# One-hot shares of an expert layer as rounded 256-column matmuls, and rounded operands in the attention scores

## The reference

```python
def one_block(args):            # attention, one block of 128 queries
    s = jnp.einsum('bhqd,bhkd->bhqk', q_blk, k).astype(jnp.float32) * scale
    s = s + c_blk[..., None] - cum[:, :, None, :]      # cum: running sum of log forget gates
    s = jnp.where(key_pos[None, :] <= q_pos[:, None], s, -jnp.inf)
    p = jax.nn.softmax(s, axis=-1)
...
s_top, i_top = lax.top_k(scores, PEER_TOPK)            # per token and head, 2 x 16 of 128 keys
...
expert_idx = jnp.take_along_axis(cand_i, pos, axis=-1) # 128 picks a token out of 128*128 experts
gates = jax.nn.softmax(best_s, axis=-1)
u_sel = u_tab[i_blk]
act = jax.nn.gelu(jnp.einsum('td,thkd->thk', h_blk, u_sel).astype(jnp.float32))
w = (g_blk * act).astype(h.dtype)
return jnp.einsum('thk,thkd->td', w, v_tab[i_blk])
```

## Time and profile before

| | |
|---|---|
| median of 3 runs | 3398.49 us (3394.14 to 3400.37) |
| profiled execution, its own time | 3398.76 us |
| its span in the trace | 3397.0 us |
| PE busy | 3303.0 us, 97% of the span |
| DVE, ACT, POOL busy | 59%, 32%, 13% |
| matmul records | 14716 |

### The profile page before, as it was taken

How to read it: one execution, slowest core, us unless ns; L and a number is a source line. 1 busy time by engine, 2 the same in 40 slices (tenths; PEclk the granted TensorE clock), 3 DMA queues, 4 the chain that set the end, 5 groups by cost and what they waited for, 6 DMA issues and landing times.

```text
span 3397.0 us, 37999 instructions
## 1 busy us (share of the span) xinstructions
PE 3303.0 (97%) x14716; PEld 2584.0 (76%) x14716; DVE 1998.6 (59%) x3778; ACT 1070.5 (32%) x1393; POOL 429.9 (13%) x186
## 2 busy tenths in 40 slices
PE   7998999989999899999989999999999999999999
PEld 6876778768777556765668888888888788888887
DVE  6678343447888789345535858566631255555554
ACT  3265222233222311234333233455542211111111
POOL 0000000014031000000002444322234100000000
PEclk9999999999999899999999999999999999999999
DMA  5144324323332333220123344388885555555553
GB/s 196 59 136 134 99 69 142 131 68 94 105 124 90 136 109 104 77 81 25 44 75 103 130 140 140 121 194 190 196 211 179 183 188 190 190 188 186 186 188 116
DMA packets 280948, 451.58 MB, mean 133 GB/s; under 512 B 147776, under 2 KB 154048, under 8 KB 280512
## 3 DMA queue, kind: packets, MB, share of 16 engines
q1 hardware_dynamic: 145152, 405.10, 36.4%
q10 hardware_dynamic: 135616, 44.04, 6.1%
HBM read 369.39 MB, written 79.69 MB: 132 GB/s over the span
## 4 chain that ended last, share of the span: by engine, by line
PE 92%; DVE 6%; ACT 1%; issue 1%; DMA 0%; POOL 0%; ACTq 0%; DVEq 0%
PE psum L588 92%; DVE wl L1372 1%; ACT wh L981 1%; DVE trigw L1469 0%; DVE yb L1583 0%; DVE psum L1725 0%; DVE lb L1574 0%; DVE trig L1470 0%; DVE trig L1465 0%; DVE cs L1581 0%; DVE y L1585 0%; DVE n L1508 0%; DVE trig L1467 0%; DVE trig L1468 0%; DVE trigw L1466 0%
## 5 line engine op out<-in xcount | busy, mean ns | idle before, releaser
L588 PE MATMUL psum<-h_hi,wh 128*128 128x512 f32 x2144 | 865.9, 404 | 45.2 <-DVE wl L1372 16.1
L1372 DVE TENSOR_TENSOR wl<-ring,wh 128x1024 fp32r<-128x1024 f32 (+2 forms) x320 | 373.6, 1171 | 850.2 <-ACT wh L981 849.3
L588 PE MATMUL psum<-h_hi,wl 128*128 128x512 f32 x2144 | 851.4, 397 | 0.0
L588 PE MATMUL psum<-h_lo,wh 128*128 128x512 f32 x2144 | 850.1, 396 | 0.0
L981 ACT ACTIVATE wh<-ring 128x1024 fp32r<-128x1024 f32 (+2 forms) x492 | 504.1, 1026 | 834.2 <-PE psum L588 813.4
L2055 POOL TENSOR_TENSOR wl<-ring,wh 128x1024 fp32r<-128x1024 f32 x172 | 426.2, 2479 | 1913.8 <-ACT wh L981 1913.8
L588 PEld LDWEIGHTS psum<-h_hi,wh 128*128 128x128 f32 x2144 | 406.3, 190 | 149.6 <-issue 54.1
L588 PEld LDWEIGHTS psum<-h_hi,wl 128*128 128x128 f32 x2144 | 405.7, 189 | 100.4
L588 PEld LDWEIGHTS psum<-h_lo,wh 128*128 128x128 f32 x2144 | 406.5, 190 | 92.8 <-issue 1.9
L588 PE MATMUL psum<-ews_hi,wl 128*128 128x512 f32 x1024 | 408.6, 399 | 0.0
L588 PE MATMUL psum<-ews_lo,wh 128*128 128x512 f32 x1024 | 403.5, 394 | 0.0
(11 more groups left out here) (367 smaller groups left out, 3825.2 us busy)
## 6 DMA issues: line engine op xcount, KB each, us to landing
ring<-tables SPq DMA_DIRECT2D x256, 512.0 KB, 3.7
acts_scratch<-ga SPq DMA_DIRECT2D x128, 256.0 KB, 2.2
gates_scratch<-stage ACTq DMA_DIRECT2D x8, 4096.0 KB, 26.7
abuf<-acts_scratch SPq DMA_DIRECT2D x128, 256.0 KB, 3.9
gbuf<-gates_scratch SPq DMA_DIRECT2D x128, 256.0 KB, 4.2
ring<-w_up SPq DMA_DIRECT2D x44, 512.0 KB, 3.6
ring<-w_modb SPq DMA_DIRECT2D x32, 512.0 KB, 3.7
statew<-states_scratch SPq DMA_DIRECT2D x16, 640.0 KB, 3.8
```

What stands on the lines that cost most here:

```text
L588: return nc.tensor.matmul(out, lhsT, rhs, start=first, stop=last, **kw)
L1372: TT(wl, slot(t, 0, size[t]), wh.bitcast(F32), ALU.subtract).then_inc(S("low_by_ve"), 1)
```

## The change

The change has these parts.

1. **Spreads.** SPREAD_AT goes from 56 to 46, SPREADS from 3 to 2, PICKS_AT to (21, 29, 36, 44). The one-hots become fp32r and unscaled, and both sets come from one DVE instruction of 1024 elements (`hots_of`). The shares are split into a rounded high part (`picks_hi`) and the rest (in `picksT`); ACT scales the one-hots of key b by both, sixteen ACTIVATEs of 128x128 for a tile (`shares_of`), into `hbg`, 256 columns a token. PE does four rounded matmuls of 256 columns for a spread, which fill two banks. DVE sums the two halves of each from PSUM into the staging tile (`stage_gates`, a reduce of 1024 elements to 512) in place of ACT's copy. ACT issues the write of a full staging tile one `ui` tile later (`park_gates`).
2. **Scores.** `cumn` is split on DVE into two rounded rows of a zeroed tile `cums`; SP moves the second by a small transfer to partitions 32 to 39; `pick_head` (128x8, a one at rows h and 32+h) stands, broadcast, for `sel`. `mask` and `ident` get rounded copies. So the second and third matmul of each block of scores are fp32r.
3. **Order in the attention loop.** `head_sum` of head hd+2 is issued behind the scores of head hd+1 instead of ahead, and writes an H bank.
4. `bank(b)` is shifted by one bank, so that the two banks of a spread stand side by side.

```diff
-SPREAD_AT, SPREADS = 56, 3
-PICKS_AT = (28, 36, 45, 54)
+SPREAD_AT, SPREADS = 46, 2
+PICKS_AT = (21, 29, 36, 44)
...
-    if _u + 2 < HEADS:
-        head_sums(HEADS + _u + 2)
     if _u + 1 < HEADS:
         scores(_u + 1)
+    if _u + 2 < HEADS:
+        head_sums(HEADS + _u + 2, "H")
...
         def bank(b, n=T):
-            return psum[:, b % NBK, 0:n]
+            return psum[:, (b + 1) % NBK, 0:n]
...
             stream("vv", "w_v2", 8)
+            sp.wait_ge(S("cum_ready"), 1)
+            sp.dma_start(cums[32:32 + HEADS, :].bitcast(F32), cum_lo[0:HEADS, :].bitcast(F32)).then_inc(S("cum_moved"), 16)
...
-                if j == SPREAD_AT + T // 4 // SPREADS + 10:
+                if j == SPREAD_AT + T // 4 // SPREADS + 6:
...
                     mm(bank(b, nk), qT[:, hd, qb * P:(qb + 1) * P], kT[:, hd, 0:nk], True, False)
-                    mm(bank(b, nk), sel[0:HEADS, hd, :], cumn[:, 0:nk], False, False)
-                    mm(bank(b)[:, qb * P:nk], ident[:, :], maskt[:, :], False, True).then_inc(PE, 1)
+                    mm(bank(b, nk), pick_head[:, hd:hd + 1].to_broadcast([P, P]), cums[:, 0:nk], False, False)
+                    mm(bank(b)[:, qb * P:nk], ident_r[:, :], mask_r[:, :], False, True).then_inc(PE, 1)
...
-                if hd + 2 < HEADS:
-                    head_sum(HEADS + hd + 2)
                 if hd + 1 < HEADS:
                     scores(hd + 1)
+                if hd + 2 < HEADS:
+                    upper_free(pe, HIGH[f"hs{HEADS + hd + 2}"])
+                    pe.wait_ge(S("hsq_ready"), HEADS + hd + 3)
+                    mm(upper(HIGH[f"hs{HEADS + hd + 2}"]), ones[:, :], ht[:, hd % 2, :], True, True).then_inc(PE, 1)
...
             def spread(n):
-                b = BLOCK[f"ui{SPREAD_AT + n // SPREADS}"] + n % SPREADS
-                block_free(pe, b)
-                pe.wait_ge(S("hot_ready"), n + 1)
-                for k in range(4):
-                    last = mm(bank(b)[:, k * P:(k + 1) * P], hot_a[:, n % 4, k * P:(k + 1) * P],
-                              hot_b[:, n % 4, k * P:(k + 1) * P], True, True)
-                last.then_inc(PE, 1)
+                b = spread_block(n)
+                for k in range(2):
+                    block_free(pe, b + k)
+                    pe.wait_ge(S("shares_ready"), 4 * n + 2 * k + 2)
+                    for q in range(2):
+                        last = mm(bank(b + k)[:, 2 * P * q:2 * P * (q + 1)], hots[n % 3][:, 2 * k + q, :],
+                                  hbg[n % 3][k][:, q, :], True, True)
+                    last.then_inc(PE, 1)
...
+            def shares_of(n):
+
+                act.wait_ge(S("hot_ready"), n + 1)
+                for q in range(4):
+                    t, one = 4 * n + q, hots[n % 3][:, 4 + q, :].bitcast(F32)
+                    to = hbg[n % 3][q // 2][:, q % 2, :]
+                    A(to[:, 0:P], one, ACT.Copy, scale=picks_hi[:, t:t + 1].bitcast(F32))
+                    A(to[:, P:2 * P], one, ACT.Copy, scale=picksT[:, 2, t:t + 1]).then_inc(S("shares_ready"), 1)
...
-                for n in SPREAD_OF[j]:
-                    gate_stage(n)
+                if j + 1 < PK:
+                    for n in SPREAD_OF[j + 1]:
+                        shares_of(n)
+                for n in SPREAD_OF[j - 1]:
+                    park_gates(n)
...
-            v.tensor_tensor_scan(cumn, ones[0:HEADS, 0:1].to_broadcast([HEADS, T]), fl[2], 0.0, ALU.mult, ALU.add)\
-                .then_inc(S("cum_ready"), 1)
+            link(v.tensor_tensor_scan(cumn, ones[0:HEADS, 0:1].to_broadcast([HEADS, T]), fl[2], 0.0, ALU.mult, ALU.add))
+            ve.wait_ge(S("cum_zero"), 1)
+            link(v.tensor_copy(cums[0:HEADS, :], cumn))
+            TT(cum_lo[0:HEADS, :], cumn, cums[0:HEADS, :].bitcast(F32), ALU.subtract).then_inc(S("cum_ready"), 1)
...
+            def hots_of(n):
+                if n >= 3:
+                    block_here(ve, spread_block(n - 3) + 1)
+                both_picks = picksT[:, 0:2, 4 * n:4 * n + 4].unsqueeze(3).to_broadcast([P, 2, 4, P])
+                TT(hots[n % 3].rearrange("p (k q) j -> p k q j", k=2),
+                   rows.unsqueeze(1).unsqueeze(1).to_broadcast([P, 2, 4, P]), both_picks, ALU.is_equal)\
+                    .then_inc(S("hot_ready"), 1)
+
+            def stage_gates(n):
...
+                block_here(ve, b + 1)
+                sums = psum[:, (b + 1) % NBK:(b + 1) % NBK + 2, :].rearrange("p b (q k j) -> p (b q) j k", k=2, j=P)
+                v.tensor_reduce(parked[g % 2][:, :, t0:t0 + 4].rearrange("p j t -> p t j"), sums, AX, ALU.add)\
+                    .then_inc(S("gates_staged"), 1)
...
+                hots_of(n)
+                if n >= 2:
+                    stage_gates(n - 2)
```

More of the change, by code:

```diff
@@ L143, in head_rows, with head_sums @@
     stage(f"hs{n}", ["B"], False, lambda k: ("qk_normed", n + 1))
-def head_sums(n):
-    stage(f"hs{n}", ["B"], False, lambda k: ("ksd_done", n - HEADS + 1))
+def head_sums(n, bank="B"):
+    stage(f"hs{n}", [bank], False, lambda k: ("ksd_done", n - HEADS + 1))
 for _u in range(NS):
@@ L190 @@
     else:
-        stage(f"ui{_j}", ["T"] + ["B"] * len(SPREAD_OF[_j]), True,
-              lambda k, j=_j: ("gates_staged", SPREAD_OF[j][k] + 1))
+        stage(f"ui{_j}", ["T"] + ["B"] * (2 * len(SPREAD_OF[_j])), True,
+              lambda k, j=_j: ("gates_staged", SPREAD_OF[j][k // 2] + 1))
 for _v in range(PK):
@@ L374, in build @@
         eq, prod = (ar(n, B + 16400 + k * 2048, 1, 2048)[:, 0, :] for k, n in enumerate(("eq", "prod")))
-        picksT = ar("picksT", B + 20496, 3)
-        hot_a, hot_b = ar("hot_a", B + 16400, 4), ar("hot_b", B + 18448, 4)
+        picksT = ar("picksT", B + 20496, 4)
+        picks_hi = ar("picks_hi", B + 22032, 1, T, F32R)[:, 0, :]
+        hots = [ar(f"hots{k}", at, 8, P, F32R) for k, at in enumerate((B + 16400, B + 17424, B + 22544))]
+        hbg = [[ar(f"hbg{k}_{j}", at, 2, 2 * P, F32R) for j, at in enumerate(ats)] for k, ats in
+               enumerate(((B + 18448, B + 18960), (B + 19472, B + 19984), (B + 23568, B + 26128)))]
         parked = [ar(f"stage{k}", B + k * PK * TG, PK, TG) for k in range(2)]
@@ L1202, in head_root @@
             def head_root(n):
-                b = BLOCK[f"hs{n}"]
-                block_here(act, b)
+                if n >= HEADS + 2:
+                    upper_here(act, HIGH[f"hs{n}"])
+                    sums = upper(HIGH[f"hs{n}"])
+                else:
+                    block_here(act, BLOCK[f"hs{n}"])
+                    sums = bank(BLOCK[f"hs{n}"])
                 act.wait_ge(S("qk_normed"), max(n - 1, HEADS))
-                A(ht[:, 2 + n % 2, :], bank(b), ACT.Sqrt, scale=1.0 / P, bias=epsc).then_inc(S("ksd_done"), 1)
+                A(ht[:, 2 + n % 2, :], sums, ACT.Sqrt, scale=1.0 / P, bias=epsc).then_inc(S("ksd_done"), 1)
             def to_head(name, n, upper_bank=False):
@@ L1321, in key_copy, with park_gates @@
                 A(scb[:, n % 4, :], bank(b), ACT.Copy).then_inc(S("sc_ready"), 1)
[L1323 to L1330, removed]
-                if t0 == TG - 4:
+            def shares_of(n):
[5 more added lines that the diff above has]
+                    A(to[:, P:2 * P], one, ACT.Copy, scale=picksT[:, 2, t:t + 1]).then_inc(S("shares_ready"), 1)
+            def park_gates(n):
+                g, last = n // (TG // 4), n % (TG // 4) == TG // 4 - 1
+                if last:
                     act.wait_ge(S("gates_staged"), n + 1)
@@ L1985, in _ @@
             ve.wait_ge(S("iota_turned"), 1)
-            def spread(n):
-                if n >= 4:
-                    block_here(ve, BLOCK[f"ui{SPREAD_AT + (n - 4) // SPREADS}"] + (n - 4) % SPREADS)
-                TT(t3(hot_b[:, n % 4, :], P), rows.unsqueeze(1).to_broadcast([P, 4, P]),
-                   picksT[:, 1, 4 * n:4 * n + 4].unsqueeze(2).to_broadcast([P, 4, P]), ALU.is_equal)
-                for q in range(4):
-                    t = 4 * n + q
-                    last = TS(hot_a[:, n % 4, q * P:(q + 1) * P], rows, picksT[:, 0, t:t + 1], picksT[:, 2, t:t + 1],
-                              ALU.is_equal, ALU.mult)
-                last.then_inc(S("hot_ready"), 1)
+            def hots_of(n):
[5 more added lines that the diff above has]
+                    .then_inc(S("hot_ready"), 1)
@@ L1997, in _ @@
+            assert spread_block(0) % 2 == 1
             for n in range(T // 4):
                 if n % (P // 4) == 0:
-                    ve.wait_ge(S("picksT_ready"), n // (P // 4) + 1)
-                spread(n)
+                    tb = n // (P // 4)
+                    at = slice(tb * P, (tb + 1) * P)
+                    ve.wait_ge(S("picksT_ready"), tb + 1)
+                    link(v.tensor_copy(picks_hi[:, at], picksT[:, 2, at]))
+                    link(TT(picksT[:, 2, at], picksT[:, 2, at], picks_hi[:, at].bitcast(F32), ALU.subtract))
+                hots_of(n)
+                if n >= 2:
+                    stage_gates(n - 2)
@@ L2002, in gated @@
```

(2 more changed lines are left out.)

32 lines of the change are left out of this document (23 added, 9 removed).

## The result

The changed kernel takes 3298.53 us (median of 4 runs, 3297.91 to 3299.58), the kernel before 3398.75 (4 runs): a ratio of 0.9709, interval 0.9697 to 0.972. That is 100.2 us less. The forecast was 3318 and the range began at 3306, so the change is faster as forecast, but by some 17 us more than its working accounts for (82.8). The profiled execution took 3299.58 us with a span of 3297.8, 99.2 less than before; what follows divides these 99.2 us.

The account below looks back on a forecast made before the run. PE was taken as the bound. From 3398.76 us, 54.2 for spreads and 28.6 for attention (23.2 + 6.9 - 1.5) gave 3316, stated as 3318 since unknowns lay rather above; range 3306 to 3342, without rivals 3308 to 3328.

Parts of the forecast that it names:

- Spreads removed and added: On PE, float32 spreads removed save 113.9 us, rounded ones added cost 59.7: gain 54.2 us, tile 6.53 us.
- ACT and DVE in the tile: Spread work stays hidden behind PE's 6.53 us tile: ACT 6.08 us with shares 0.29 apart, DVE 4.9 with staging 1.22.
- (a): Rival: DVE becomes the bound of the spreads with a staging of 2.3 us; +33, 3351 us; chance 0.12.
- (b): Rival: ACT becomes the bound, its short ACTIVATEs 0.38 us apart without overlap; +76, 3394 us, no change; chance 0.04.
- (c): Rival: slower than before, ACT's shares at 0.40 us make a tile 8.04 us; 3412 us; chance 0.03.
- The distance at which PE begins to wait: Distance between ACT's shares above which PE waits: about 0.34 us once, about 0.32 in steady state.
- Attention's matmuls: Rounded forget terms and masks in the scores cost 1.12 us a head instead of 4.24; 2.9 taken, eight heads 23.2 us.
- the switches of type: In the scores, 0.05 to 0.1 us for each switch between float32 and rounded matmuls, lowering 3.1 us a head to 2.9.
- The move of the sum: In the attention loop, the 1.15 us gap goes in six turns, 6.9 us; 1.5 us allowed for later waits.
- rival (d): Attention gains only its matmuls' half: DVE's chain sets the turn at 15.5 us, not 13.8; 3329 us; chance 0.13.
- the half clock beside head 0's scores: Half clock over 1522 to 1538 follows a PE gap that stays; may give one or two us more or fewer.
- The `vo` stage and the first block unchanged to 1 us: Sign in the changed profile: these two stretches, outside the changed work, keep their length to 1 us.

Follow-up runs that it names:

- experiment 9: The kernel before with parts two and three of the change (scores, attention order), its spreads as before: 3351.35 us, ratio 0.9869.
- experiment 10: The changed kernel with four of a tile's sixteen ACT shares each done in two halves of 64 columns: 3320.92 us.
- experiment 11: The changed kernel with eight of a tile's sixteen ACT shares each done in two halves of 64 columns: 3368.82 us.
- experiment 2: The changed kernel with forget terms and mask on the same 128-row operands, but read as float32 instead of rounded: 3309.31 us, ratio 0.9746.
- experiment 3: The kernel before with only its forget term on 128 rows as float32, with the three new tiles that come with it: 3371.88 us, ratio 0.9919.
- Experiment 4: The changed kernel with head 0's forget term alone in float32 on 8 rows: 3309.27 us, ratio 0.9735.
- experiment 7: The changed kernel with its three new tiles declared behind the arena instead of ahead of it: 3309.02 us, ratio 0.9741.
- experiment 5: The kernel before with an unused tile of 264 words ahead of the arena, a shift of 1056 bytes: 3390.48 us, ratio 0.9974.
- experiment 6: The kernel before with an unused tile of 8 words ahead of the arena, a shift of 32 bytes: 3389.94 us, ratio 0.9978.
- experiment 1: The changed kernel without its second part: forget terms and mask in float32 as before, without the three new tiles: 3339.12 us, ratio 0.9834.
- experiment 12: The changed kernel with DVE copying the last head's `probsT` ahead of its two other jobs: 3291.28 us, ratio 0.9682.

## Why the prediction was right or wrong

- **Spreads removed and added: right.** 54.2 us forecast, 53.6 shown by experiment 9 against the changed kernel. The tile is 6.52 us, so the price of a rounded matmul of 256 columns and the absence of a cost for switching hold.
- **ACT and DVE in the tile: right.** 0.29 apart, `stage` 1.22 us, no wait of PE. Experiments 10 and 11 show the point where ACT takes over, so rivals (a), (b) and (c) fell for the reason given against them. (The distance at which PE begins to wait once, (7.2 - 0.2 - 1.44)/16, is 0.35 and not 0.34; nothing hung on it.)
- **Attention's matmuls: right in kind, 0.4 us a head too small.** I took 2.9 us a head and the scores gave 3.31. The step was that the forget terms are 0.1 us longer each than q-k and the mask 0.33 by nature, so that 2.52 us of q-k stay. Experiments 2 and 3 show that both, and a part of q-k's time, are the eight rows: 0.39 us a block. With 128 rows q-k takes 2.16 us a head. What was added came out as taken: the scores of head 0 last from 1520.49 to 1523.76, 3.27 us, which leaves 1.11 for the forget terms and masks against 1.12, with nothing over for the switches of type, for which some 0.2 had been put in. (In the turns 0.18 us more lie ahead of `ht`.)
- **The move of the sum: right in the changed kernel, for half of the reason.** The gap of 1.15 went and rival (d) did not come. But PE's new waits for DVE, 1.7 us for `probs` and 0.9 for `probsT`, are 2.6 us where 1.5 were allowed. The 0.41 us a head more from the scores, seven times, less this 1.1, make 1.8 of the 2.0 us by which the turns beat the forecast; two errors of opposite sign met there. That without the bank of its own another 1.56 us a turn would have been lost, I had not seen.
- **The step that failed** is the sentence on the half clock beside head 0's scores, that it "follows a gap on PE ahead of them that the change leaves; it may give one or two us more or fewer". The gap of 1.78 us is in both kernels and the half clock is not. Of nine profiles with 128 rows at head 0 (float32 or rounded, shifted or not, the sum ahead or behind) eight show full clock there and one 3.4 us at half; of the five with eight rows each shows 13.7 to 17.1 us at half. Experiment 4 prices it: 10.7 us in the medians, 8.7 in the profile up to the first transposes, with the 8-row matmuls' own time. It isn't the chance of one profiled execution: over whole executions the mean clock was 0.986 to 0.988 in every one of the five kernels with eight rows there, and 0.989 to 0.991 in every one of the other nine, but for two of experiment 7 at 0.988.
- **Not in the sum at all:** "The `vo` stage and the first block unchanged to 1 us". `vo` became 3.1 us shorter and the tiles 2.5, by the addresses, 5.6 in the profiles. Experiments 5, 6 and 7 show it in both directions; in medians the shift alone is worth 8.5, 7.5 and 10.5 us, the part beyond 5.6 being small shares ahead of the gelus and falls of the clock that move with them. Without it, the changed kernel takes 3309.0, within the range given.

The balance in the profile: 82.8 forecast, -0.6 spreads, +2.0 turns, +8.4 at head 0, +5.6 addresses, +1.0 behind the transposes: 99.2.

Open are two things. One is by what property the few rows bring the half clock: it was only shown that it goes with the rows and neither with float32 nor with the length of the scores. The rows are not the whole of it either. In the one kernel with 128 rows that fell (experiment 7) the clock fell 0.70 us behind the first matmul of the scores; in the kernel before and in experiment 1 it fell 0.70 and 0.73 us behind it, while the first 8-row matmul was still running. In these three the rows can hardly have started the fall; what differs is its length, 3.4 us against 17.1 and 13.7. In experiments 4, 5 and 6 it fell 1.6 to 2.1 us behind it. The other is what in the address costs the 0.02 us a tile.

## What to carry to other kernels

When a change touches a place that runs at half clock, price both cases from the trace, the fall gone and the fall staying: a gap that stays does not mean that the fall does. An operand with few rows between full ones can cost more than its columns; widen it with zeros when that is free, and measure. Before giving a microsecond to an edit that adds tiles, run the kernel before with an unused tile of that size: here it was worth 5.6 of 99 us in the profiles, and 7.5 to 10.5 in the medians.

## What the runs showed of the hardware

- A float32 matmul of 8 rows between ones of 128 rows costs 0.39 us more for the three of a block than the same with 128 rows (1.05 against 0.66 at 128 columns). With it behind a gap of 1.78 us, the granted clock went to 0.50 (1.2 GHz) for 13.7 to 17.1 us in five of five profiles; with 128 rows behind the same gap it stayed at 1.00 (2.4 GHz) over head 0's scores in eight of nine, and was 0.50 for 3.4 us in the ninth.
- A wait of PE of 3.94 us ahead of `mixed` came with 6.8 us at 0.50; with the wait cut to 0.29 us the clock stayed at 1.00 (experiment 12).
- A float32 matmul of 128 columns takes 0.22 us. A rounded mask of 128 columns has 0.06 us from its start to the next one's (1573.54 to 1573.60) in the second and third block of a turn and 0.12 in the first, but between float32 matmuls these distances don't add up: the 1.11 us of a head's rounded forget terms and masks are what 0.12 for 128 columns gives, with any cost of switching in it. (The Trainium skill, TensorE: Matmul & The Clock Gate, section Back-to-back issue gap, gives N/2.4 + 2.5 ns for an isolated matmul, 56 ns at 128 columns. The one distance agrees with it, the block does not; and at 256 columns show 117 ns, not 109.)
- Shifting everything in the arena, the matmuls' operands among it, by 32 bytes changed the stretch behind the last gelu from 723.0 to 719.9 us, with the same instructions.
